# Eight modulation units moved from the second layer's attention projections into the first layer's output projection

## The reference

```
mods = jnp.einsum('bd,lde->lbe', jax.nn.silu(c), ada_w) + ada_b[:, None, :]
for i in range(DEPTH):
    sh_m, sc_m, g_m, sh_f, sc_f, g_f = jnp.split(mods[i][:, None, :].astype(x.dtype), 6, axis=-1)
    h = rms_norm(x, norm_w[i, 0]) * (1 + sc_m) + sh_m
    ...  # the mixer: layer 0 SSD heads and windowed attention, layer 1 gated DeltaNet and block attention
    x = x + g_m * rms_norm(y, norm_w[i, 1])
    h = rms_norm(x, norm_w[i, 2]) * (1 + sc_f) + sh_f
    y = conv_ffn(h, ffn_w_up[i], ffn_conv_w[i], ffn_conv_b[i], ffn_w_down[i])
    x = x + g_f * rms_norm(y, norm_w[i, 3])
```

## Time and profile before

| what | value |
|---|---|
| median of 3 runs | 1168.77 us (1168.54 to 1171.28) |
| time of the profiled execution | 1168.98 us |
| its span | 1167.2 us |
| PE busy | 1065.2 us (91%) |
| DVE busy | 799.1 us (68%) |
| ACT busy | 612.6 us (52%) |
| mean granted TensorE clock | 0.957 of full |

### The profile page before, as it was taken

How to read it: one execution, slowest core, us unless ns; L and a number is a source line. 1 busy time by engine, 2 the same in 40 slices (tenths; PEclk the granted TensorE clock), 3 DMA queues, 4 the chain that set the end, 5 groups by cost and what they waited for, 6 DMA issues and landing times.

```text
span 1167.2 us, 26335 instructions
## 1 busy us (share of the span) xinstructions
PE 1065.2 (91%) x9487; PEld 966.0 (83%) x9487; DVE 799.1 (68%) x1716; ACT 612.6 (52%) x1370; POOL 2.9 (0%) x5
## 2 busy tenths in 40 slices
PE   5899878969999999999999778799999999999997
PEld 4799757957789999888999677689966779999876
DVE  0587333767588888887888557545744998888854
ACT  2566525335576666447666633433234457666544
POOL 0000000000000000000000000000000000000000
PEclk8899889988999999999999878899999999999999
DMA  9667325742666665973676333023101684666662
GB/s 355 221 180 236 109 107 217 281 172 77 205 226 182 184 186 178 329 248 95 216 236 199 106 126 92 24 69 93 57 1 57 215 288 129 180 182 182 183 189 90
DMA packets 55114, 195.57 MB, mean 168 GB/s; under 512 B 6099, under 2 KB 8147, under 8 KB 54908
## 3 DMA queue, kind: packets, MB, share of 16 engines
q1 hardware_dynamic: 55036, 194.49, 51.0%
HBM read 193.39 MB, written 1.07 MB: 167 GB/s over the span
## 4 chain that ended last, share of the span: by engine, by line
PE 78%; DVE 10%; ACT 4%; DMA 3%; issue 2%; SPq 1%; DVEq 0%; ACTq 0%
PE proj L526 53%; PE acc L526 24%; DVE w_lo L1546 2%; DMA ada_long<-in_ada_stream 2%; DMA ada_first<-in_ada_stream 1%; SPq L427 1%; ACT w_hi L1134 1%; DVE yn L1700 1%; PE acc L758 1%; DVE x L1707 1%; ACT k_junk L1389 1%; DMA ada_ssd<-in_ada_stream 1%; DVE ada_sum L1561 0%; DVE mmat L1857 0%; DVE dec L1944 0%
## 5 line engine op out<-in xcount | busy, mean ns | idle before, releaser
L1546 DVE TENSOR_TENSOR w_lo<-raw,w_hi 128x512 fp32r<-128x512 f32 x528 | 358.5, 684 | 135.2 <-ACT w_hi L1134 133.3
L1134 ACT ACTIVATE w_hi<-raw 128x512 fp32r<-128x512 f32 x528 | 327.3, 624 | 169.8 <-PE acc L526 117.6
L526 PE MATMUL proj<-h_hi,w_hi 128*128 128x256 f32 x1408 | 406.5, 289 | 2.5 <-DVE w_lo L1546 2.0
L526 PE MATMUL proj<-h_lo,w_hi 128*128 128x256 f32 x1408 | 403.5, 287 | 4.5 <-DVE h_lo L1754 4.3
L526 PE MATMUL proj<-h_hi,w_lo 128*128 128x256 f32 x1408 | 402.4, 286 | 0.0
L526 PEld LDWEIGHTS proj<-h_hi,w_hi 128*128 128x128 f32 x1408 | 274.9, 195 | 6.5 <-issue 3.9
L526 PEld LDWEIGHTS proj<-h_lo,w_hi 128*128 128x128 f32 x1408 | 274.7, 195 | 6.6 <-DVE h_lo L1754 6.6
L526 PEld LDWEIGHTS proj<-h_hi,w_lo 128*128 128x128 f32 x1408 | 274.5, 195 | 0.0
L526 PE MATMUL acc<-w_hi,a_hi 128*128 128x512 f32 x304 | 122.8, 404 | 4.6 <-DVE w_lo L1546 2.2
L526 PE MATMUL acc<-w_lo,a_hi 128*128 128x512 f32 x304 | 120.8, 397 | 0.0
L526 PE MATMUL acc<-w_hi,a_lo 128*128 128x512 f32 x304 | 120.2, 395 | 0.0
(11 more groups left out here) (289 smaller groups left out, 1305.7 us busy)
## 6 DMA issues: line engine op xcount, KB each, us to landing
raw<-in_w_stream SPq DMA_DIRECT2D x264, 512.0 KB, 3.6
ada_long<-in_ada_stream SPq DMA_DIRECT2D x40, 512.0 KB, 6.9
ada_ssd<-in_ada_stream SPq DMA_DIRECT2D x24, 512.0 KB, 5.4
ada_first<-in_ada_stream SPq DMA_DIRECT2D x20, 512.0 KB, 4.8
ada_out<-in_ada_stream SPq DMA_DIRECT2D x12, 512.0 KB, 4.7
hankel<-bias_scratch SPq DMA_DIRECT2D x2, 1024.0 KB, 5.8
x<-in_x_tiles SPq DMA_DIRECT2D x1, 1024.0 KB, 10.1
cst<-in_constants SPq DMA_DIRECT2D x1, 864.0 KB, 5.3
```

The lines of the kernel that those rows point to most:

```text
L526: return pe.matmul(out, a, b, start=start, stop=stop, skip_group_check=True)
L1134: act.activation(hi, src, ACT.Copy).then_inc(w_rounded, 1)
L1546: dve.tensor_tensor(lo, src, hi.bitcast(F32), ALU.subtract).then_inc(w_split, 1)
```

## The change

The eight units 72 to 79 are summed in `out0`, steps 6 to 13, as two groups of four, two terms in each step. Nothing of them is left in `q1`, `k1` and `v1`. The other units keep their place. The stream of modulation units in memory is reordered so that the eight come in front of those of `down0` (`ADA_ORDER`), and so the numbers in the code shift: 52 to 59 are now the moved units, and 60 to 79 are what 52 to 71 were.

```
-ADA_WITH = {"down0": 52, "q1": 72, "k1": 76, "out1": 80, "down1": 92}
+ADA_WITH = {"out0": 52, "down0": 60, "out1": 80, "down1": 92}
+ADA_ORDER = [*range(52), *range(72, 80), *range(52, 72), *range(80, 96)]
-ADA_GROUPS = [range(m, m + 4) for m in range(52, 72, 4)] + [range(m, m + 2) for m in range(72, ADA_UNITS, 2)]
+ADA_GROUPS = [range(m, m + 4) for m in range(52, 80, 4)] + [range(m, m + 2) for m in range(80, ADA_UNITS, 2)]
-        ADA_AFTER = {("down0", 20): 68, ("q1", 3): 72,
-                     ("k1", 1): 74, ("k1", 3): 76, ("v1", 1): 78, ("down1", 3): 92, ("down1", 4): 94}
+        ADA_AFTER = {("out0", 11): 52, ("out0", 14): 56, ("down0", 20): 76, ("down1", 3): 92, ("down1", 4): 94}
         def k_tail(name, k):
+            if name == "out0":
+                return not 6 <= k < 14
-            stream(n_z0 + 17, n_up0 + 4)
-            for m in range(52, 60):
+            stream(n_z0 + 17, n_out0 + 6)
+            sp.wait_ge(d_gated, SSD_G)
+            for k in range(4):
+                load_ada(52 + k)
+                load_ada(56 + k)
+                load_w(n_out0 + 6 + k)
+            stream(n_out0 + 10, n_up0 + 4)
+            for m in range(60, 68):
                 load_ada(m)
-            for m in range(72, 76):
-                stream(n_q1 - 20 + 4 * (m - 72), n_q1 - 16 + 4 * (m - 72))
-                load_ada(m)
-            stream(n_q1 - 4, n_q1 + 4)
-            for k in range(4, 8):
-                load_w(n_q1 + k)
-                load_ada(72 + k)
-            stream(n_q1 + 8, n_out1 + 6)
+            stream(n_q1 - 20, n_out1 + 6)
-                    ada_with("v1", k)
-                    pe.wait_ge(mods_read, 4)
+            pe.wait_ge(mods_read, 3)
             keep_busy(0, "up0", 5)
-                        if name == "down0":
-                            m, t = ADA_WITH[name] + j // 4 * 4, 2 * (j % 4)
+                        if name in ("out0", "down0"):
+                            j0 = j - 6 if name == "out0" else j
+                            m, t = ADA_WITH[name] + j0 // 4 * 4, 2 * (j0 % 4)
                             ada_term(m, t, i)
                             halves.pop(0)()
                             ada_term(m, t + 1, i)
                             halves.pop(0)()
-                if name == "down0":
-                    read_mods(52, 72, PB[0])
-                    make_gain(1, 0, 3)
-                    make_gain(1, 1, 3)
+                if name == "out0":
+                    read_mods(52, 60, PB[3])
+                elif name == "down0":
+                    read_mods(60, 80, PB[0])
+                    make_gain(1, 0, 4)
+                    make_gain(1, 1, 4)
-                    read_mods(72, 80, PB[3])
```

More of the change, by code:

```diff
@@ L51 @@
 ADA_QUADS = 13
-ADA_WITH = {"down0": 52, "q1": 72, "k1": 76, "out1": 80, "down1": 92}
-ADA_GROUPS = [range(m, m + 4) for m in range(52, 72, 4)] + [range(m, m + 2) for m in range(72, ADA_UNITS, 2)]
+ADA_WITH = {"out0": 52, "down0": 60, "out1": 80, "down1": 92}
+ADA_ORDER = [*range(52), *range(72, 80), *range(52, 72), *range(80, 96)]
+ADA_GROUPS = [range(m, m + 4) for m in range(52, 80, 4)] + [range(m, m + 2) for m in range(80, ADA_UNITS, 2)]
 ADA_SUMMED = range(4 * ADA_QUADS, ADA_UNITS)
-ADA_RINGS = {range(0, 16): 8, range(16, 28): 4, range(28, 52): 4, range(52, 72): 8, range(72, 80): 4, range(80, 92): 6, range(92, 96): 8}
+ADA_RINGS = {range(0, 16): 8, range(16, 28): 4, range(28, 52): 4, range(52, 80): 8, range(80, 92): 6, range(92, 96): 8}
 PRM, PRM_COLS = {}, 0
@@ L357, in build @@
         quad_rows = lambda i: (PB[2 - i % 2] if i < 4 else PB[3])[:, P * (i % 2 + 1):P * (i % 2 + 2)]
-        ada_buffer = lambda p: (ada_pairs if 72 <= ADA_GROUPS[p][0] < 92 else ada_sum)[:, p % 2]
+        ada_buffer = lambda p: (ada_pairs if 80 <= ADA_GROUPS[p][0] < 92 else ada_sum)[:, p % 2]
         ada_group = lambda m: next(p for p, q in enumerate(ADA_GROUPS) if m in q)
@@ L384, in build @@
         G_ROWS = (g_low, g_low, g_high, g_low)
-        ADA_BANK = {"down0": PB[0], "q1": PB[3], "k1": PB[3],
-                    "v1": PB[3], "out1": PB[1], "down1": PB[2]}
-        ADA_AFTER = {("down0", 20): 68, ("q1", 3): 72,
-                     ("k1", 1): 74, ("k1", 3): 76, ("v1", 1): 78, ("down1", 3): 92, ("down1", 4): 94}
+        ADA_BANK = {"out0": PB[3], "down0": PB[0], "out1": PB[1], "down1": PB[2]}
+        ADA_AFTER = {("out0", 11): 52, ("out0", 14): 56, ("down0", 20): 76, ("down1", 3): 92, ("down1", 4): 94}
         for k in (5, 7, 9, 11, 13, 14):
@@ L393, in build @@
         for k in range(5, 20, 4):
-            ADA_AFTER["down0", k] = 52 + k - 5
+            ADA_AFTER["down0", k] = 60 + k - 5
         def k_tail(name, k):
+            if name == "out0":
+                return not 6 <= k < 14
             if name == "out1":
@@ L487, in _ @@
                 if k >= 4:
-                    load_ada(56 + k)
+                    load_ada(64 + k)
             for k in range(8, 12):
                 load_w(n_down0 + 8 + k)
-                load_ada(60 + k)
+                load_ada(68 + k)
             stream(n_down0 + 20, n_q1 - 20)
@@ L1669, in read_mods @@
                 m = mods[:, :, :, :].rearrange("p l s k -> p (l s k)")
-                dve.tensor_tensor(m[:, a:b], bank[:, a:b], prm[:, PRM["ada_b"] + a:PRM["ada_b"] + b], ALU.add).then_inc(mods_read, 1)
+                t = slice(ADA_ORDER[a], ADA_ORDER[a] + b - a)
+                dve.tensor_tensor(m[:, t], bank[:, a:b], prm[:, PRM["ada_b"] + t.start:PRM["ada_b"] + t.stop], ALU.add).then_inc(mods_read, 1)
             def make_gain(layer, which, mods_at):
@@ L2214 @@
         + mixer_units(cd, ZT, GQ_T, 8, 6144, 4608, 0, 6168, 7192) + [out_units(v["cd_w_out"][0])] + ffn_units(1), axis=1))
-    ada_stream = np.ascontiguousarray(np.concatenate([unit_columns(v["ada_w"][layer], 0, 48) for layer in range(2)], axis=1))
+    ada_stream = np.ascontiguousarray(np.concatenate([unit_columns(v["ada_w"][layer], 0, 48) for layer in range(2)], axis=1)[:, ADA_ORDER])
     prm = np.concatenate([v[k].reshape(-1, P) for k in ("c", "ada_b", "norm_w", "ssd_conv_w", "ssd_conv_b", "ssd_norm_w",
```

## The result

The changed kernel is slower: 1173.49 us as the median of 20 runs (1169.36 to 1176.51), beside 1169.87 us (1165.46 to 1175.92) for 20 runs of the kernel before on the same chips. The ratio is 1.0031, 95% interval [1.0020, 1.0043]. I had forecast 1166.2 us. The profiled execution took 1175.1 us, with a span of 1173.3 us.

What follows compares the result with a forecast made beforehand. TensorE carries 78% of the chain; VectorE counts only between links in `q1` to `v1`. Removed 4.1 us, added 2.0 in `out0`, clock gain 0.5: -2.6 us, from 1168.77 to 1166.2 us, range 1162.6 to 1169.8.

Steps and rivals of the forecast that it cites:

- (a): Gates after `q1` unit 0: ScalarE's idle behind two VectorE terms goes, 0.68 us gained.
- (b): Decay tails after `q1` unit 2: ScalarE's wait behind terms goes, 1.06 us gained.
- (c): Keys after `q1` unit 3: the two terms ahead of `k_tok` go entirely, 0.84 us gained.
- (d): TensorE's four pair sums in `q1`, `k1`, `v1`: only the second lies in a TensorE-bound stretch, 0.36 us gained.
- (e): Values after `k1` unit 3: split and `v_tok` no longer stand behind two terms, 1.2 us gained.
- (i): Twelve modulation transfers in `out0` ahead of weight units 6 to 9: cost 0, by a margin of 9 us.
- rival of late weights: `out0` weight units 7 to 9 queue behind eight modulation transfers, TensorE waits 8.5 us: 1174.7 us; chance 0.10.
- covered terms: Rival: half of the attention stage's 4.1 us is found again as another wait, no clock gain: 1168.7 us; chance 0.15.
- (g): Two TensorE sums of four units in `out0`, behind units 11 and 14, 0.79 us each: 1.6 us added.
- (f): `out0` step 6: one first term ahead of the late VectorE split adds 0.4 us; the other 15 terms cost nothing.
- clock step: Shorter pauses in the attention stage give TensorE's clock between 0 and 2.5 us; 0.5 us of gain taken.
- the first: Rival: a slow-clock stretch at `q1` unit 3 disappears, 2.5 us in place of 0.5: 1164.2 us; chance 0.25.

Runs made afterwards that it cites:

- four edited versions: Changed kernel with scan pauses filled (1167.22 us), one matmul ahead of the scan (1175.34), units 92 to 95 as one group (1171.5), or filling plus that group (1165.85).
- late group: Changed kernel with units 92 to 95 summed as one group of four in steps 12 to 15 of `down1`, not two pairs: 1171.5 us, ratio 1.0013.
- removal: Kernel before without the terms and sums of units 72 to 79 in `q1`, `k1` and `v1`, transfers kept: 1170.93 us, ratio 0.9997; with scan pauses filled 1164.77 us.
- last pair: Changed kernel and kernel before, each with scan pauses filled and units 92 to 95 as one group late in `down1`: 1165.85 and 1168.36 us.
- addition: Kernel before plus an unused copy of the eight transfers, 16 terms and two sums in `out0`, attention stage as before: 1173.35 us, ratio 1.0023.
- shifted: Changed kernel with one unread matmul of 256 columns in dense TensorE work ahead of the second layer's scan, pauses left open: 1175.34 us, ratio 1.0039.
- before with filled pauses: Kernel before with two unread matmuls (512 and 256 columns) in the pauses at the second layer's scan start: 1170.59 us, ratio 1.0007.

## Why the prediction was wrong

**Where it was right.** (a) 0.68 us: the gates gained 0.67. (b) 1.06: gained 1.04 (1.71 - 0.67). (c) 0.84: 1.19 (2.90 - 1.71), with a slow piece of 5.36 us in place of 5.64 ahead of it. (d) and (e), 1.56 together: 1.29 (4.19 - 2.90). Sum 4.19 against 4.1. (h), (i): 0 as said. The rival of late weights did not come up: the piece of 36 matmuls behind the first split is 8.49 us as before. The covered terms did not either.

**Sizes that were off.** (g) was 2 x 0.79 and measured 2 x 0.89, since the matmuls behind a sum start 0.1 us later than in an unbroken piece. (f) was 0.4 and measured 0.6 in the changed kernel's two traces. But the stretch of (f), from 232 to 295 us, also holds slow pieces of 256 to 270 us that stand ahead of the terms and differ from kernel to kernel. Against the first trace of before it is +0.6, +0.7, +2.4, +2.4, +2.4 and -1.1 us long in the six traces with the change, and between -1.0 and +0.1 us in the five further ones without these terms. The means are +1.2 and -0.4 (the latter of six, with the first trace of before). With these, 3.4 us would be lost in `out0` in place of 2.0. Likewise the attention stage won 5.0 us in the changed kernel's traces and 4.0 to 4.6 in the four edited versions. Stretches with slow pieces in them move like this; the two sums agree to 0.02 us in the traces of the change, and `up0` and `down0` from end to end to 0.02 us in all thirteen.

**The clock step, the one that failed.** I wrote that it gives "between 0 and 5.64 - 3.14 = 2.5 us" and took 0.5. That was right for the stage that I looked at: it gained 0.7 us more than the terms, with the piece at 738 us. What failed is that I had treated the clock as a matter of the changed stage alone and put it at nothing for every stage behind. I had also put into the text that it would be wrong "if its slow-clock pieces change their number". One did go, the piece at 738 us. But the number of such pieces changed further back too, where nothing had been altered. The bounds of this step should have reached below zero by the price of a slow piece that appears, 6.55 - 3.76 = 2.8 us for that piece alone. In place of a gain of 0.5 us the clock gave back 4.4 us in the scan and 1.6 us in `down1`. None of my rivals was that; the first says that the clock could fall the other way, but for a part of a stretch in the changed stage and within the range.

**What is shown.** The scan's loss is the clock and not a wait: the waits and the instructions are the same, the matmuls longer. The two pauses ahead are needed for it: filling them takes it away in the three kernels that have it and were tried (changed, changed with the late group, removal), shifting the program by 0.8 us does not. With the loss away, the changed kernel is 6.3 us (of 1173.49) to 7.5 us (of 1174.71) faster, at 1167.22, and beats the kernel before. So it is this, and in part `down1`, that turned a gain into a loss of 3.6 us. How large the gain is by itself is not settled, as the last pair above shows.

**Why the same two pauses make the clock fall in one kernel and not in the other.** The change touches nothing in the 80 us ahead. Time since the start is not it: the second traces of both kernels reach the first unit of `out1` at the same 821.99 us, and only the changed one falls; the kernel with the removal alone reaches it at 819.86 us and falls too. But in each of the thirteen traces all changes of the granted clock lie on one row of evenly spaced moments (to 0.01 us), and against the start this row stands elsewhere from trace to trace. Carried on through the scan it tells the kernels apart. In the three traces with open pauses and no fall (before, twice, and the addition) such a moment lies between the two pauses, 0.1 to 0.2 us behind the first. In the five with the fall no moment lies between them: one lies 0.5 to 0.6 us inside the first pause (changed, twice, and late group) or 0.1 to 0.5 us ahead of it (shifted, removal), and the fall comes at the next, inside or behind the second pause. With filled pauses the changed kernel stands at the same place as without, to 0.1 us, and does not fall.

That place is made by the attention stage. Counted from the last such moment ahead of each landmark, the six traces with the change reach the third unit of `q1` after 1.2 to 2.3 us, and the fourth unit of `z1` all after 1.5 us. The five with the old attention stage come in at 2.3 to 3.3 us and leave at 0.6 to 0.7 us, and the two with the removal leave at 1.9 and 2.1 us. So a stage with slow pieces in it takes up the scatter of the start and passes the program on at a place that goes with its own code. The Trainium skill's page TensorE: Matmul & The Clock Gate, section "What's actually happening", says that the chip's watch over TensorE runs on by itself and doesn't start anew with a kernel. The thirteen traces agree with it. That this place decides on the fall is argued from eight traces with open pauses; no run moved the changed kernel to the place of the one before.

**What stays open.** In `down1` the kernels sort the same way: of the eight with the two pairs there, three have the fall (changed, changed and shifted, before with filled pauses), and they reach its third unit 0.4 to 1.5 us behind such a moment, the others 1.9 us or more. But no run tests it there. How much of the 2.5 to 3.4 us is the worth of the move itself is open as well.

## What to carry to other kernels

A gain inside a stage can be given back where a later stage no longer passes its pauses at full clock. Compare stage by stage, from fixed landmarks, down to the end, and look for pieces with the same matmuls and other lengths. Where two short pauses stand close together, put a matmul that nobody reads into each; here 0.7 us of it saved 5.8 us in the changed kernel's scan. And where one edit's worth is to be known, measure it also in kernels in which such falls are filled, and look in both traces for falls elsewhere: the plain comparison said +0.3% and the filled ones -0.3 and -0.4% of the same change, the latter with a fall in one of the two kernels.

## What the hardware showed that I had not expected

- From `q1` on the slow stretches are no noise. Two traces of one kernel have them at the same instructions, behind a start that differed by 0.6 to 1.0 us, and their lengths agree to 0.01 us (6.55 and 6.56 us at the scan, 34.67 twice in `down1`).
- A piece of 32 small matmuls at the same place takes 3.76 us in one kernel and 6.55 in another, although the instructions and the pauses ahead (1.3 and 0.8 us) are the same.
- Added matmuls of 512 and 256 columns cost 0.7 us and took two slow pieces away, the second of them 53 us later.
- The clock of TensorE changes only at evenly spaced moments that are not tied to the program, and the attention stage with its slow pieces leaves the program at 1.5 us behind one of them in all six traces with the change, at 0.6 to 0.7 us in the five with the old code.
- A sum of four units, 8 single-column matmuls in the rows, takes 0.79 us by its own row and 0.89 us by what stands around it.
